# A two-layer transformer kernel: the first mixer's attention scored by pairs of heads in plain fp32

## The reference, cut to what matters

```
q: 8 heads of 64, k and v: 2 heads of 64 (a group of 4 query heads shares one)
for the 4 blocks of 128 tokens:  keys = previous, own and next block (masked to |distance| <= 128), and 256 context keys
for the 2 blocks of 128 context tokens:  keys = the 256 context keys
p = softmax([q.k / 8 over the keys, sink of the head])       # the sink has no value row
out = p[keys] @ v
```

## Time and profile before

| | us |
|---|---|
| median of 3 runs (lowest, highest) | 3332.19 (3329.98, 3333.5) |
| the profiled execution | 3335.83 |
| its span in the trace | 3334.0 |
| PE busy | 3213.6 (96%) |
| DVE, ACT, POOL busy | 2242.9, 1229.4, 88.1 |

### The profile page before, as it was taken

The page is one execution under the profiler, slowest core; times in us unless marked ns, Lnnn a source line. Parts: engine busy times, 40 slices in busy tenths (PEclk is TensorE's granted clock), DMA queues, the critical chain, the costliest instruction groups (busy, mean ns, idle before and its releaser), DMA issues. The chain is left out here.

```text
span 3334.0 us, 50499 instructions
## 1 busy us (share of the span) xinstructions
PE 3213.6 (96%) x20310; PEld 2950.6 (88%) x20310; DVE 2242.9 (67%) x3826; ACT 1229.4 (37%) x2088; POOL 88.1 (3%) x189
## 2 busy tenths in 40 slices
PE   8999999988999999989999999989999999999999
PEld 7999999977889999989999999877888878877777
DVE  4979896477577777777777776664333666566654
ACT  4111112356553343364433343553222432334332
POOL 0000000001100000000000000000000000000000
PEclk9999999999999999999999999999999999999999
DMA  5545553200122222232222221112323421122232
GB/s 220 188 170 179 186 181 120 76 27 26 50 82 68 88 83 83 95 79 67 77 92 83 96 91 68 52 48 82 96 95 100 129 76 34 61 81 69 70 102 95
DMA packets 95287, 313.82 MB, mean 94 GB/s; under 512 B 11424, under 2 KB 15712, under 8 KB 93520
## 3 DMA queue, kind: packets, MB, share of 16 engines
q1 hardware_dynamic: 88128, 290.04, 25.9%
q0 software_dynamic: 6928, 20.55, 2.2%
HBM read 300.06 MB, written 4.19 MB: 91 GB/s over the span
## 5 line engine op out<-in xcount | busy, mean ns | idle before, releaser
L665 PE MATMUL psum<-zh,wh 128*128 128x384 f32 (+2 forms) x2384 | 774.1, 370 | 30.3 <-DVE sx L3693 7.9
L635 ACT ACTIVATE wh<-raw 128x512 fp32r<-128x512 f32 (+3 forms) x551 | 447.4, 817 | 849.3 <-PE psum L665 461.4
L665 PE MATMUL psum<-zh,rawl 128*128 128x384 f32 (+2 forms) x2384 | 751.7, 361 | 0.0
L665 PE MATMUL psum<-zl,wh 128*128 128x384 f32 (+2 forms) x2372 | 748.6, 361 | 0.0
L645 DVE TENSOR_TENSOR rawl<-raw,wh 128x512 fp32r<-128x512 f32 (+3 forms) x551 | 502.6, 927 | 252.5 <-ACT wh L635 251.2
L665 PEld LDWEIGHTS psum<-zh,wh 128*128 128x128 f32 x2384 | 439.9, 191 | 85.1 <-issue 34.3
L1136 PE MATMUL psum<-formq,wh 128*128 128x386 f32 x1848 | 479.9, 341 | 13.8 <-DVE formq L944 4.8
L665 PEld LDWEIGHTS psum<-zh,rawl 128*128 128x128 f32 x2384 | 442.0, 191 | 42.6
L665 PEld LDWEIGHTS psum<-zl,wh 128*128 128x128 f32 x2372 | 440.3, 191 | 41.3 <-issue 2.9
L1136 PEld LDWEIGHTS psum<-formq,wh 128*128 128x128 f32 x1848 | 337.4, 189 | 20.0 <-DVE rawl L645 6.7
L748 DVE SCALAR_TENSOR_TENSOR h<-psum,mod,h 128x512 f32<-128x512 f32 (+1 forms) x288 | 169.9, 627 | 191.5 <-PE psum L665 191.1
(11 more groups left out here) (491 smaller groups left out, 4512.2 us busy)
## 6 DMA issues: line engine op xcount, KB each, us to landing
raw<-in_wup SPq DMA_DIRECT2D x176, 512.0 KB, 4.2
modw<-in_mod_w SPq DMA_DIRECT2D x128, 512.0 KB, 3.6
raw<-in_w_sw SPq DMA_DIRECT2D x36, 512.0 KB, 3.5
raw<-in_wdn SPq DMA_DIRECT2D x64, 256.0 KB, 4.0
raw<-in_wdn SPq DMA_DIRECT2D x32, 448.0 KB, 3.4
adaw<-in_ada_w SPq DMA_DIRECT2D x8, 1024.0 KB, 16.1
raw<-in_wdn SPq DMA_DIRECT2D x16, 512.0 KB, 3.9
raw<-in_od_in SPq DMA_DIRECT2D x16, 512.0 KB, 3.4
```

The costliest lines, as they stand in the source:

```text
L635: nc.scalar.activation(hi_of(n, i), x, ACT.Copy).then_inc(w_hi, 1)
L665: last = nc.tensor.matmul(psum[:, at + to:at + to + e - s], w[:, q * P:(q + 1) * P], x[:, q, s:e], start=(q == 0 and j == 0), stop=(q == s ...
```

## The change

The keys are no longer split, nor the queries: `kh`, `kl`, `zq` and the instructions that make them on ACT, DVE and POOL go, and the scores are plain fp32 matmuls over the 64 partitions of the head, straight from `ev`. The two heads of a pair are scored together, the even one from the upper half of the partitions, the odd one from the lower half: each has its local keys in a bank of its own (PSUM columns 1536 minus their number up, or 2048 up), and both have their context keys in the bank between (columns 1536 to 2048), the odd one after the even one is done there (`ctx_done`). The loops run over 24 pairs (`EPAIRS`, p) instead of 48 units: in a step PE scores pair p, does the chunks of the old turn 2p, the values of pair p-2, turns the first unit of pair p-1, does the chunks of turn 2p+1 and turns the second unit of pair p-1. ACT starts a step's exponentials when the maxima of both units are there, and does both before the copies. DVE takes both maxima, then divides. There is one place for scores throughout. The probabilities have two pairs of buffers (`ev_s`, `ev_s_odd`). The turned probabilities now have columns 2560 to 3200 and the output 3200 to 3328: the fifth tile of 128 turned columns shares the bank of the output, and before it PE waits for the copy-out of the pair before (`at_o`).

```diff
-        zq = sb("zq", ZQ_AT, [4, P], f32r)
-        kh = sb("kh", FM_AT, [2, T], f32r)
-        kl = sb("kl", R_AT, [2, T], f32r)
-        ev_s = sb("ev_s", SCR_AT, [2, 640])
+        ev_s = [sb("ev_s", SCR_AT, [2, 640]), sb("ev_s_odd", FM_AT, [2, 640])]
...
-        E_SUM, E_SPR, E_ROT, E_VT, E_S, E_PT, E_OUT, E_MIX = 3584, 2048, 3072, 2048, 1024, 2048, 3072, 3584
+        E_SUM, E_SPR, E_ROT, E_VT, E_PT, E_OUT, E_MIX = 3584, 2048, 3072, 2048, 2560, 3200, 3584
+        E_CTX = 1536
...
-            for i, u in enumerate(EUNITS):
-                if i < 4:
-                    pool.wait_ge(eq_hi, EQ_HI)
-                else:
-                    pool.wait_ge(at_pc, i - 3)
-                nc.gpsimd.tensor_tensor(u.place[u.beside], u.query, u.place[u.r], ALU.subtract).then_inc(zq_lo, 1)
...
-                self.keys = [((kh[:, g, TX:T], kl[:, g, TX:T]), 256, 256)]
-                if self.local:
-                    near = slice(lo * P, (hi + 1) * P)
-                    self.keys.append(((kh[:, g, near], kl[:, g, near]), 512, self.local))
-                self.own_s = 1024 if u < SECOND_S or u % 2 else 0
+                ctx, near = ev[r, KROW + g, TX:T], ev[r, KROW + g, lo * P:(hi + 1) * P]
+                if hd % 2 == 0:
+                    self.c0, at = E_CTX + 256, E_CTX + 512
+                    self.keys = [(ctx, self.c0, 256)] + [(near, at, self.local)] * (n < 4)
+                else:
+                    self.c0 = at = E_CTX - (self.local if n < 4 else 384)
+                    self.keys = [(near, at, self.local), (ctx, E_CTX, 256)] if n < 4 else [(ctx, at, 256)]
                 self.masks, self.mask_pe = None, []
-                if u >= SECOND_S:
-                    self.mask_pe = [(512, 0)] * (0 < n < 4) + [(512 + (n > 0) * P + P, P)] * (n < 3)
+                if u >= MASK_PE:
+                    self.mask_pe = [(at, 0)] * (0 < n < 4) + [(at + (n > 0) * P + P, P)] * (n < 3)
...
-            def scores(self, c, w):
-                return psum[:, self.own_s + c:self.own_s + c + w]
+            def scores(self):
+                return psum[:, self.c0:self.c0 + self.w]
             def probs(self):
-                return ev_s[:, self.u % 2, 0:self.w]
-        SECOND_S = 32
+                return ev_s[self.u // 2 % 2][:, self.u % 2, 0:self.w]
+        MASK_PE = 32
         EUNITS = [EvenUnit(12 * m + 2 * n + j, 2 * m + j, n) for m in range(4) for n in range(6) for j in range(2)]
+        EPAIRS = [EUNITS[i:i + 2] for i in range(0, len(EUNITS), 2)]
         NE = total["u"] = len(EUNITS)
+        NEP = len(EPAIRS)
...
-            pe.wait_ge(ek_lo, EK_LO + 2)
+            pe.wait_ge(e_rope, 6)
...
-            def score(i):
-                u = EUNITS[i]
-                pe.wait_ge(zq_lo, i + 1)
-                if i == SECOND_S:
-                    pe.wait_ge(drained, all_drained(EU))
-                elif i:
-                    pe.wait_ge(at_e, i if i < SECOND_S else i - 1)
-                for (k_hi, k_lo), c, w in u.keys:
-                    masks = u.mask_pe if c == 512 else []
-                    nc.tensor.matmul(u.scores(c, w), u.place, k_hi, start=True, stop=False)
-                    last = nc.tensor.matmul(u.scores(c, w), u.place, k_lo, start=False, stop=not masks)
-                    for at, m in masks:
-                        last = nc.tensor.matmul(u.scores(at, P), ident[:], ev_mask[:, m:m + P], start=False,
-                                                stop=(at, m) == masks[-1])
-                last.then_inc(at_qk, 1)
-            def transposes(i):
-                u = EUNITS[i]
-                pe.wait_ge(at_p, i + 1)
-                if i >= 1:
-                    pe.wait_ge(at_pc, i)
+            def score(p):
+                pair = EPAIRS[p]
+                if p:
+                    pe.wait_ge(at_e, 2 * p)
+                for j in range(len(pair[0].keys)):
+                    for u in pair:
+                        k, c, w = u.keys[j]
+                        own = [c <= at < c + w for at, _ in u.mask_pe]
+                        if j and c == E_CTX:
+                            pe.wait_ge(ctx_done, p + 1)
+                        last = nc.tensor.matmul(psum[:, c:c + w], u.query, k, start=True, stop=not any(own))
+                        if j == 0 and u is pair[0]:
+                            last.then_inc(ctx_done, 1)
+                for u in pair:
+                    for at, m in u.mask_pe:
+                        last = nc.tensor.matmul(psum[:, at:at + P], ident[:], ev_mask[:, m:m + P], start=False,
+                                                stop=(at, m) == u.mask_pe[-1])
+                last.then_inc(at_qk, 2)
+            def transposes(u):
+                pe.wait_ge(at_p, u.u + 1)
+                if u.u >= 1:
+                    pe.wait_ge(at_pc, u.u)
                 for j in range(len(u.vals)):
+                    if j == 4 and u.u >= 2:
+                        pe.wait_ge(at_o, u.u // 2 * 2)
                     last = nc.tensor.transpose(psum[:, E_PT + j * P:E_PT + (j + 1) * P],
                                                u.probs()[:, j * P:(j + 1) * P], ident[:])
                 last.then_inc(at_t, 1)
...
-            for i in range(SECOND_S + 1):
-                score(i)
-                chunks_pe(pe, run, chunks_at(i))
+            def beside_units(i):
                 if i in VV_SUM:
                     vv_sums(pe, VV_SUM[i])
-                if i >= 3 and i % 2:
-                    values(i - 3)
-                if i >= 1:
-                    transposes(i - 1)
                 if i in VV_STEPS:
                     vv_rows_pe(pe, VV_STEPS[i])
-            score(SECOND_S + 1)
-            for i in range(SECOND_S + 1, NE + 2):
-                if i + 1 < NE:
-                    score(i + 1)
-                if i % 2:
-                    values(i - 3)
-                if i <= NE:
-                    transposes(i - 1)
                 if i in MIX_STEPS:
                     mix_pe(pe, MIX_STEPS[i])
+            for p in range(NEP + 2):
+                if p < NEP:
+                    score(p)
+                chunks_pe(pe, run, chunks_at(2 * p))
+                if p >= 2:
+                    values(EPAIRS[p - 2])
+                if 1 <= p <= NEP:
+                    transposes(EPAIRS[p - 1][0])
+                beside_units(2 * p)
+                chunks_pe(pe, run, chunks_at(2 * p + 1))
+                if 1 <= p <= NEP:
+                    transposes(EPAIRS[p - 1][1])
+                beside_units(2 * p + 1)
...
+            def copy_turned(u):
+                act.wait_ge(at_t, u.u + 1)
+                if u.u >= 2:
+                    act.wait_ge(at_pv, u.u // 2 * 2)
+                nc.scalar.activation(ev_pt[:, u.u % 2, 0:u.w], psum[:, E_PT:E_PT + u.w], ACT.Copy).then_inc(at_pc, 1)
+            for p in range(NEP + 2):
+                if p < NEP:
+                    act.wait_ge(at_s, EPAIRS[p][1].u + 1)
+                for u in EPAIRS[p] if p < NEP else ():
+                    nc.scalar.activation(u.probs(), u.scores(), ACT.Exp, bias=nmx[:, u.k:u.k + 1],
                                          scale=er[:, u.factor:u.factor + 1],
                                          accum_out=rsum[:, u.k:u.k + 1]).then_inc(at_e, 1)
                     nc.scalar.activation(esink[:, u.k:u.k + 1], cols[:, SINK + u.hd:SINK + u.hd + 1], ACT.Exp,
                                          bias=nmx[:, u.k:u.k + 1]).then_inc(at_sink, 1)
-                if 1 <= i < NE - 3:
-                    act.wait_ge(at_qk, i)
-                    query_hi(i + 3)
-                if 1 <= i <= NE:
-                    u = EUNITS[i - 1]
-                    act.wait_ge(at_t, i)
-                    if i >= 3:
-                        act.wait_ge(at_pv, (i - 1) // 2 * 2)
-                    nc.scalar.activation(ev_pt[:, u.u % 2, 0:u.w], psum[:, E_PT:E_PT + u.w], ACT.Copy).then_inc(at_pc, 1)
-                if i >= 3 and i % 2:
-                    u = EUNITS[i - 3]
-                    act.wait_ge(at_pv, i - 1)
+                if p >= 2:
+                    u = EPAIRS[p - 2][0]
+                    act.wait_ge(at_pv, u.u + 2)
                     nc.scalar.activation(u.pair_out, psum[:, E_OUT:E_OUT + P], ACT.Copy).then_inc(at_o, 2)
+                for i in (2 * p, 2 * p + 1):
+                    if 1 <= p <= NEP:
+                        copy_turned(EPAIRS[p - 1][i % 2])
+                    beside_act(act, run, i, chunks_at(i))
...
-            for i in range(NE + 2):
-                if SECOND_S <= i < NE:
-                    maximum(i)
-                if 1 <= i <= NE:
-                    divide(i - 1)
-                if i < SECOND_S:
-                    maximum(i)
-                if i - 1 in VV_STEPS:
-                    vv_rows_dve(dve, VV_STEPS[i - 1])
-                if i - 1 in MIX_STEPS:
-                    mix_dve(dve, MIX_STEPS[i - 1])
-                beside_dve(dve, run, i, chunks_at(i - 1) if i else 0)
```

(57 more changed lines are left out.)

22 lines of the change are left out of this document (7 added, 15 removed).

## The result

The changed kernel takes 3367.26 us (median of 4 runs, 3364.77 to 3370.53), the kernel before 3331.64 beside it: ratio 1.0105, 95% interval 1.0092 to 1.0117. It is 35.6 us slower; forecast were 3355 and +23.5. The profiled execution took 3364.77 us, its span is 3363.0.

What follows compares the result with a forecast made beforehand. PE nearly sets the pace while chunks last, then DVE. Front -4.4, steps +8.5 and +11.4, switches +3, clock +5 give +23.5 on 3335.83 = 3359.3; 3.6 lower for the median, said as 3355 us, range 3338 to 3374.

Steps and rivals of the forecast that it cites:

- The front: Start of the attention: without split keys and queries, first scores start at about 688.0 instead of 692.44, -4.4 us.
- Scores: PE's score matmuls of a pair: 1.28 us for 640 keys, 1.07 for 512, 0.64 for 256, halves partly overlapping.
- rival 1: Pair scores on PE: the two row halves do not run at once, +13.6 us, 3369; chance 0.17.
- The chain X: From a pair's scores through DVE to ACT's last exponential: 6.75 us for 640 keys, 5.87 for 512, 3.88 for 256.
- Losing the second place: Steps 16 to 22, without chunks: DVE's work now waits in turn, 49.55 us against 38.18, +11.4.
- the clock's term, +5: Work behind PE's gaps in steps 0 and 18 to 21 runs at 1.2 GHz: between 0 and 17 us, taken as +5.
- my lists': Step times summed: steps 0 to 15 134.0 us against 125.5, +8.5; steps 16 to 22 49.55 against 38.18, +11.4.
- switches: PE entering another array shape for scores: 0.17 us each, 48 entries and exits, 0 to 7 us, taken as +3.
- Rival 2: Steps 18 to 23: clock stays at 1.2 GHz throughout, +7 and some at the tail, 3366; chance 0.12.
- signs of being wrong: PE waiting for DVE's probabilities only, steps 18 to 22 under 6.5 us each, or a shorter stretch with chunks.
- Rival 3: Both attention stretches: PE's queue decides every step, first loses up to 8 us, second 2, 3318; chance 0.07.
- Rival 4: Whole change: list counts waits twice, worth 12 us, switches and clock cost nothing, 3335 to 3337; chance 0.07.

Runs made afterwards that it cites:

- unpaired plain fp32: The kernel before with plain fp32 scores straight from `ev`, unit by unit in the old order and banks: 3351.86 us, ratio 1.006.
- order experiment: The changed kernel with a pair's score matmuls issued unit by unit instead of alternating between the row halves: 3369.27 us, ratio 1.0107.
- filled gaps: The changed kernel with extra unread matmuls only where PE idled, in steps 0, 3, 8, 14 and 18 to 21: 3355.63 us, ratio 1.0065.

## Why the prediction was right, and where it was not

**The front** was right: 688.0 forecast, 688.09 seen, and the experiment with it alone gains 3.3 us, with the interval above.

**Scores** were right. 1.28 us and a gap of 0.17 were forecast for a pair of 640 keys, and 708.24 to 709.68 is 1.44; rival 1 wanted 2.13. Two units of 256 keys did better than forecast: 0.63 us with the gap, where I had 0.64 and the gap. A single such unit also takes 0.63 (unpaired plain fp32), so these overlap wholly. The reason that I gave, that the halves overlap only where the heads alternate, fell with the order experiment. The Trainium skill (TensorEngine Tiling (Array Packing), Key Properties) says that different tiles can load and multiply in parallel; the trace agrees, with 1.44 us for two units where one alone takes 1.27. Pairs with 512 keys take 1.44 as well, where I had 1.07 and the gap; a single one takes 1.06.

**The chain X** was right: 6.75 forecast for 640 keys, 6.80 in step 2. What stands behind it, copy-out, fifth tile, copy, second turn, stands there in the order forecast, and PE's idle time ahead of turns, 30.1 us over all its groups, is just 30, not "well over" it.

**Losing the second place** was right as a mechanism: 10.4 us measured for it in the kernel before. My +11.4 for steps 16 to 22 was for all that stands in these steps, and with filled gaps (clock 0.97) they take 53.65 us, 15.5 more than before, so the agreement of 11.4 with 10.4 is in part luck.

**The step that failed is the clock's term, +5.** The steps add up to 142.25 and 61.10 us against my lists' 134.0 and 49.55: 19.8 over, where 3 for switches and 5 for the clock stood. Filling the gaps brings back 12.8 of it, so the clock cost some 13 us, not 5. The steps themselves show it: 18 to 21 are 9.0 us over the list in the change, and 2.4 over it with the gaps filled; steps 2, 5 to 7, 9, 10 and 12, where the clock stayed up, are all within 0.3 us of it. With a clock of 12.8 the sum is +31.3. Of the 35.3 seen in the trace 4 are left: 1.6 for eight pairs of 512 keys that take 0.2 us longer than I had them, and 2.4 for switches beyond my 3 or errors of the list. The switches had a slip too: 48 times 0.17 us is 8.2, not 7, and no run measures how much of it is on the path. I had looked for a low clock in steps 0 and 18 to 21 and priced only the work on the path in the steps with the gap. In the trace it is low also around 728, 768 and 820 us, in the first stretch, where PE is busy most of the time, and it slows the chunks and scores of the following step too. Rival 2 had the mechanism and nearly the time (3366), but in steps 18 to 23 alone, which is not where all of it lay: 5.4 of the 12.8 us came back in the first stretch. The mistake in method was to price the clock by the length of the gaps, not by all that runs behind them. That 3355 came within 12 us of 3367 all the same owes to the front and the list, which hold at full clock. One of my signs of being wrong was set badly: step 22 took 6.22 us, under the 6.5 that I named, but my own list had 5.8 for it.

**Rival 3** failed as the sum said: both stretches got longer. **Rival 4** fell with it.

**The rest of the span.** The projection behind the attention starts 36.1 us later (901.15 against 865.05), as the medians have it, while the profiled spans differ by 29.0. Nearly all of the missing 7 us lies in two later stages with the same code, which vary from trace to trace: between the first and the last use of `fhidh` lie 1001.5 us in the trace before, 998.0 in the one after and 998.2 to 1001.5 in the experiments; for `ox` 133.8, 129.8 and 129.8 to 132.2. The trace before is at the upper end of both, the one after at the lower.

**Left open.** Why pairs of 512 keys take as long as those of 640. Why the clock stayed at 0.50 for 23.7 us of a busy PE in the kernel with unpaired plain fp32. Starting the first exponential early while both units share a bank was not tried, nor the fifth tile without its wait: two engines would use one bank at once.

## What to carry to other kernels

Doing two units at once on one engine does not shorten a chain whose other engines take them one after the other; it makes every step as long as the chain, and it takes the place in which the next unit could have been scored. Before such a change, write down what stands between two scores on every queue, as a sum per step: here that gave the structure of the loss to within some 4 us, once the clock was priced from a run. Then price the clock by everything that PE runs after a gap. If gaps must stay, a few matmuls that nobody reads are worth trying in the gaps only: here they gave back 13 us, 7.5 of them in the steps without chunks, and only 4.0 there when they also stood in steps that had no gap.

## What the runs showed of the hardware

- Plain fp32 matmuls on the two halves of the rows overlap whatever the order in which they are issued: 1.44 us for two units of 640 keys in either order, against 1.27 for one; 0.63 for two units of 256 keys and for one.
- A granted clock of 0.50 can outlast its gap by far: in the kernel with unpaired half-row scores it stood from 829.7 to 853.4 us while PE was busy 23.69 of 23.70 us, behind a gap of 2.18 us. In the kernel before it was 0.50 from 822 to 824 and 1.00 again in the windows from 825 on. Why, no run tells. A PE that is slow is also a busy PE, so its busy share doesn't show a low clock.
- The clock's price shows behind the gap: PE did nothing from 691.9 to 696.1, the clock fell within that gap, and it was 0.50 in the window from 698 to 702, while PE was busy all the time.
